# Softmax attentions: scores of unit u+2 ahead of the transposes of unit u on TensorE

## What is computed

```
# layer 0, "differential": 8 heads of 2 x 64 columns
logits = einsum(q, k) + bias                 # two score matrices per head
p = softmax(logits);  attn = p[:, 0] - lam * p[:, 1]
o = rms_norm(attn @ v)                       # then @ w_o
# layer 1, "forgetting" (FoX): 16 heads of 64 columns
logits = einsum(q, k) + (c[t] - c[s])        # causal
o = softmax(logits) @ v                      # then @ w_o
```

## Time and profile before

| | |
|---|---|
| median of 3 runs | 2606.8 us |
| the profiled execution's own time | 2606.01 us |
| its span, first to last instruction | 2604.2 us |
| TensorE busy | 2499.6 us, 96% |
| VectorE, ScalarE, GpSimd busy | 50%, 29%, 62% |
| granted TensorE clock, mean | 0.987 |
| first attention, its units | 1292 to 1497 us |
| FoX attention, its units | 1955 to 2188 us |

### The profile page before, as it was taken

How to read it: one execution, slowest core, us unless ns; L and a number is a source line. 1 busy time by engine, 2 the same in 40 slices (tenths; PEclk the granted TensorE clock), 3 DMA queues, 4 the chain that set the end, 5 groups by cost and what they waited for, 6 DMA issues and landing times. The chain is left out here.

```text
span 2604.2 us, 37103 instructions
## 1 busy us (share of the span) xinstructions
PE 2499.6 (96%) x12731; PEld 2062.8 (79%) x12744; DVE 1310.3 (50%) x2044; ACT 752.0 (29%) x1399; POOL 1614.5 (62%) x1548
## 2 busy tenths in 40 slices
PE   9989999999999999999999899999999999999998
PEld 7878888888877888888777677888877777778886
DVE  8667666443424433321454558775163334777722
ACT  3445453001232121100334533332032222433300
POOL 8646555765445777777544267887763334788874
PEclk9999999999999999999999999999999999999999
DMA  5323323432222333323322123332222221333331
GB/s 163 98 79 112 97 82 103 124 85 66 69 65 101 94 96 97 97 97 96 107 63 68 37 81 89 97 97 97 86 78 82 69 65 49 89 89 96 97 99 63
DMA packets 235791, 229.22 MB, mean 88 GB/s; under 512 B 15808, under 2 KB 228288, under 8 KB 235672
## 3 DMA queue, kind: packets, MB, share of 16 engines
q1 hardware_dynamic: 212224, 204.72, 26.3%
q10 hardware_dynamic: 23448, 22.84, 3.1%
HBM read 225.29 MB, written 4.84 MB: 88 GB/s over the span
## 5 line engine op out<-in xcount | busy, mean ns | idle before, releaser
L583 POOL TENSOR_SCALAR whi<-raw 128x512 fp32r<-128x512 f32 x772 | 561.9, 728 | 899.1 <-issue 488.0
L585 POOL TENSOR_TENSOR wlo<-raw,whi 128x512 fp32r<-128x512 f32 x772 | 1054.3, 1366 | 64.5
L625 PE MATMUL PS<-opA_hi,whi 128*128 128x512 f32 x1872 | 747.1, 399 | 11.4 <-DVE fu L1927 4.3
L625 PE MATMUL PS<-opA_hi,wlo 128*128 128x512 f32 x1872 | 732.2, 391 | 0.0
L625 PE MATMUL PS<-opA_lo,whi 128*128 128x512 f32 x1872 | 731.8, 391 | 0.0
L625 PEld LDWEIGHTS PS<-opA_hi,whi 128*128 128x128 f32 x1872 | 353.6, 189 | 99.5 <-issue 16.1
L625 PEld LDWEIGHTS PS<-opA_hi,wlo 128*128 128x128 f32 x1872 | 353.1, 189 | 75.4
L625 PEld LDWEIGHTS PS<-opA_lo,whi 128*128 128x128 f32 x1872 | 353.7, 189 | 71.0 <-issue 1.5
L1937 DVE SCALAR_TENSOR_TENSOR facc<-fu,vec,facc 128x512 f32<-128x512 f32 x176 | 206.2, 1230 | 44.9 <-ACT facc L1321 44.6
L619 PE MATMUL PS<-whi,opA_hi 128*128 128x256 f32 x704 | 207.0, 294 | 0.0
L619 PE MATMUL PS<-whi,opA_lo 128*128 128x256 f32 x704 | 200.3, 284 | 0.0
(11 more groups left out here) (306 smaller groups left out, 3298.4 us busy)
## 6 DMA issues: line engine op xcount, KB each, us to landing
raw<-in_w_in_dram SPq DMA_DIRECT2D x184, 256.0 KB, 2.7
raw<-in_ffn_w_in_dram SPq DMA_DIRECT2D x176, 256.0 KB, 2.7
raw<-in_ffn_w_out_dram SPq DMA_DIRECT2D x88, 256.0 KB, 2.6
raw<-in_a_w_qkv_dram SPq DMA_DIRECT2D x48, 256.0 KB, 2.7
raw<-in_w_ffn_gate_dram SPq DMA_DIRECT2D x44, 256.0 KB, 2.7
raw<-in_w_ffn_up_dram SPq DMA_DIRECT2D x44, 256.0 KB, 2.7
raw<-in_w_ffn_down_dram SPq DMA_DIRECT2D x44, 256.0 KB, 2.6
acs_row<-acs_dram ACTq DMA_DIRECT2D x16, 512.0 KB, 5.7
```

Source lines behind the costliest of these rows:

```text
L583: nc.gpsimd.tensor_scalar(whi[slot][:], raw[raw_slot][:], 1.0, 1.0, ALU.mult, ALU.mult).then_inc(w_high, 1)
L585: nc.gpsimd.tensor_tensor(wlo[slot][:], raw[raw_slot][:], whi[slot][:].bitcast(F32), ALU.subtract).then_inc(slab_split, 1)
L625: last = nc.tensor.matmul(psum_fm(key, panel, m), a, b[:, k, :], start=k + n == 0, stop=k == total - 1 and n == 2)
```

## The change

In `order2` the step S(u+2) is moved ahead of T(u) (in FoX ahead of W(u-1) and T(u)). No instruction is added or removed.

```diff
             if u < 31:
                 out.append(("M", u + 1))
 
-            out += [("W", u - 1)] * (u > 0 and names[0] == "q3") + [("T", u)]
             if u < 30:
                 out.append(("S", u + 2))
+            out += [("W", u - 1)] * (u > 0 and names[0] == "q3") + [("T", u)]
             out += [("W", u - 1)] * (u > 0 and names[0] != "q3")
             if u < 31:
                 out.append(("D", u + 1))
```

## The result

| | before | changed |
|---|---|---|
| median of 7 runs, us | 2606.8 | 2619.1 |
| lowest and highest, us | 2606.1, 2608.1 | 2612.3, 2623.2 |
| span of the profiled run, us | 2604.2 | 2618.7 |
| granted TensorE clock, mean | 0.987 | 0.980 |

The ratio is 1.0044, with a 95% interval from 1.0035 to 1.0054: 12.3 us slower at the medians, where 4.8 were forecast, and outside the range that was given (to 2616.5). The kernel also became uneven: its runs spread over 10.9 us, those of before over 2.0 here and up to 7.0 when it was timed more often later. Each run comes with its mean granted clock, and the two go together: 2612.3 us at 0.984, 2616.1 at 0.982, 2619.1 at 0.981, 2623.2 at 0.979.

The account below looks back on a forecast made before the run. TensorE, busy 96% of the span, was taken as the bound, so the change only moves waits: -9.8 + 3.15 + 2.75 + 0.55 + 2.1 + 3.0 + 3.05 = +4.8 us, forecast 2611.6, range 2605.0 to 2616.5.

Parts of the forecast that it names:

- (a): FoX where no slab follows V(u-1): S(u+2) fills T's wait for W(u-1), 8 x 0.72 = 5.8 us less.
- (b): FoX, after an X with no slab behind it: T's three waits for ScalarE's copy go, 2.1 us less.
- (c): First attention, u = 7, 15, 23: S(u+2) fills T's wait for ScalarE's copy, 3 x 0.63 = 1.9 us less.
- (d): First attention, u = 6, 14, 22: later T(u-1) delays M(u+1) through ScalarE's root, S(u+2) waits, 3.15 us more.
- (e): u = 0: S(2) waits for M(1) ahead of the warm-up; 2.75 us more in the first attention, 0.55 in FoX.
- the case with the clock back: First rival: at u = 0 the clock recovers as before, costing 1.2 us there; 2610.1 us in all, chance 0.20.
- (f): Around u = 25: S(27) waits uncovered for M(26), delaying warm-up and T(25); 2.1 us more first attention, 3.0 FoX.
- (g): u = 27 to 29, both attentions: no slab hides T's copy once S goes first, 3.05 us more in all.
- The second rival: Clock falls at FoX's end for one or two stretches: 1.3 to 3.4 us more, 2612.9 to 2615.0, chance 0.30.
- its sign for the place: FoX's end: one stretch granted 0.5 between 2148 and 2160 would decide for the second rival.
- The rule of the Trainium skill: Small idle times between matmul groups make the clock go back and forth; for the middle of FoX given nothing.

Follow-up runs that it names:

- the whole change filled: The changed kernel, all orders and waits kept, with TensorE's new waits filled by warm-up matmuls: 2608.4 us, 10.7 less than the changed kernel.
- the run of units 27 to 29: Against the kernel before, S(u+2) ahead of T(u) only for u = 27, 28, 29 of both attentions: 2613.8 us, ratio 1.0026.
- the middle only: Against the kernel before, S(u+2) ahead of T(u) only for u = 1 to 23 of both attentions: 2595.2 us, ratio 0.9958.
- the ends: Against the kernel before, S(u+2) ahead of T(u) only for u = 0 and 24 to 29 of both attentions: 2630.3 us, ratio 1.0092.
- with S(27)'s wait filled: S(u+2) ahead only for u = 24 and 25, warm-up matmuls ahead of S(27) and FoX's V(24): 2617.5 us; the same without filling: 2617.1.
- with the next wait filled as well: The kernel with units 24 and 25 reordered and filled, plus seven warm-up matmuls ahead of T(26) in FoX: 2612.9 us, ratio 1.0023.
- FoX and behind an X: Against the kernel before, S(u+2) ahead for u = 1 to 23 of FoX and u = 7, 15, 23 of the first attention: 2592.8 us.
- unit 0 filled: Against the kernel before, S(2) ahead of T(0) only, both attentions, its wait filled by 5 or 2 warm-up matmuls: 2606.9 us, ratio 1.0001.
- that of the Y units: Against the kernel before, S(u+2) ahead of T(u) only for u = 5, 13, 21 of the first attention: 2609.5 us, ratio 1.0013.
- the one of all but those: Against the kernel before, S(u+2) ahead for u = 1 to 23 of both attentions except 5, 13, 21 of the first: 2593.0 us.

## Why the prediction was wrong

The direction was right and the places were; the size was not. Step by step:

- **(a), (b)**, waits of T in FoX: forecast -7.9, measured -9.85 from V(4) to V(23). Right in kind. Each place gave 0.69 to 0.96 where its wait had been 0.69 or 0.72. In unit 5 the steps themselves also take less: from the start of S to the slab 1.55 us (2013.76 to 2015.31), where from the start of T it was 1.71 (2001.26 to 2002.97). The units with nothing to fill gave some 0.05 each; that this has the same reason is not shown.
- **(c)**, behind an X: forecast 3 x 0.63, measured 3 x 0.83 or 0.84.
- **(d)**, the Y units: forecast 3 x 1.05, measured 3 x 1.24 from V(5) to V(6). The chain is shown by two kernels.
- **(e)**, u = 0: forecast 2.75 and 0.55, measured 2.78 and 1.74. The low clock went on in both attentions. I took that for the first attention, by the row from 1459.30, and left it out for FoX, where the same reasoning held. With the wait filled the costs are 1.07 and 0.2 to 0.36, near the 1.2 and 0.55 of the case with the clock back; but in the whole change filled FoX had 1.90 all the same, so a filled wait did not always bring the clock back there.
- **(f)**, u = 24 to 26: the step that failed. "M(26) then ends at 2145.75, S(27) with masks 1.2, warm-up 1.5" priced everything behind the new wait with durations at full clock. The chain of delays it describes is right: 2.29 for 2.1 in the first attention, 2.8 for 3.0 in FoX (with its waits filled), wherever the clock stayed full. In the changed kernel it did not: V(25) of the first attention came 4.96 later and not 2.1, and in FoX V(27) lost 8.85 against V(23), 3.0 of it forecast here and 0.6 in (g).
- **(g)**, u = 27 to 29: forecast 3.05 in all; the changed kernel has 1.2 in the first attention and in FoX 0.64 and 0.73 at V(28) and V(29). At V(27) of FoX the low clock covers it; from the last matmul of the slab to V(27) it is 0.37 (3.00 us for 2.63). That is 2.9 in all. The run of these units alone has 1.85 in the first, 3.6 in all. Right, if a little low.

The second rival named what happened, the low clock at the end of FoX, and its sign for the place. Two things were wrong with it. It was priced at one or two stretches, 1.3 to 3.4 us; four came there, and 8.85 less 3.0 and 0.37 is 5.5 us. And it was named for FoX alone: the first attention got two more at u = 25, under a wait of 1.74 that I had put at 1.6 and charged as a delay only. I judged the clock by the one wait of 1.47 in FoX behind which it stayed full; the run of units 27 to 29 shows that the same wait can also be followed by the low clock, so that row carried less than I took from it. The rule of the Trainium skill (page "TensorE: Matmul & The Clock Gate", section "A second HAM failure mode: psum-queue depth-cycling") that I set aside for the middle of FoX was rightly set aside there, with the clock at 1.00 before and after: its waits of 0.72 had cost no clock, and filling them gained no more than their length and 0.24. At FoX's end the trace agrees with it: waits of 0.6 to 2.1 us stand close together, and what was lost was work at half clock between them. Which waits do this, the runs here do not settle.

Left open: why a given wait is followed by the low clock in one kernel and not in another, and the 1.7 us behind the attentions, where single stretches of low clock moved to other places.

## What to carry to other kernels

A step that waits should not be put ahead of the work that covers its wait; here seven filler matmuls stood exactly there, and moving the waiting step past them uncovered the wait, delayed the filler, and had both run at half clock. Where a reorder is good in steady state, apply it there alone and keep the first and last units as they are: the middle gave 11.7 us, the ends took 23.4. And when a new idle time of TensorE is priced, price what stands behind it at half clock too, several times over if more waits follow within a few us.

## What was not expected of the hardware

- Adding useless matmuls made the changed kernel 10.7 us faster (2619.1 to 2608.4), with the order of its steps kept.
- Filling one wait can hand the low clock to the next: with S(27)'s wait filled, the first stretch at half clock at FoX's end came at 2155.5 and not at 2150.2 us, behind the next wait, and the kernel was no faster (2617.5 against 2617.1); only with the next wait filled as well was it 2612.9.
- Kernels that do the same at unit 26 of FoX got the clock at 1.00 or at 0.51 behind the same wait of 1.47 or 1.48 us. The kernel before had it full, and so had the middle only, FoX and behind an X, and unit 0 filled; the run of units 27 to 29, that of the Y units and the one of all but those had it low. From V(26) to the last matmul of the slab it was 4.34 us in those four and 5.93 to 5.98 in these three. So the kernel at 2593.0 still holds a stretch at half clock that has nothing to do with its own order:

```profile
2137.40:2140.80 3.40, 3.40 (x15) 3.11 (x15) 0.02 (x1) 1.11 (x2) 0.00 (x0) 0.51 0.02 5
```
